# Gate and up by Strassen's seven products, the second norm moved behind the output projection, and the feed-forward in the same program

## The reference, cut to what matters

```python
h = x + mixed @ w_out
gu = rms_norm(h, norm2) @ w_gate_up        # 1024 -> 2 * 2816
gate, up = jnp.split(gu, 2, axis=-1)
return h + (jax.nn.silu(gate) * up) @ w_down
```

## Time and profile before

| | us |
|---|---|
| median of three runs | 3157.95 (3147.9 to 3160.55) |
| the profiled execution's own time | 3149.9 |
| its span, first to last instruction | 3148.2 |
| PE busy | 2934.9 (93%) |
| DVE, ACT, POOL busy | 1575.6, 1087.4, 353.3 |

### The profile page before, as it was taken

How to read it: one execution, slowest core, us unless ns; L and a number is a source line. 1 busy time by engine, 2 the same in 40 slices (tenths; PEclk the granted TensorE clock), 3 DMA queues, 4 the chain that set the end, 5 groups by cost and what they waited for, 6 DMA issues and landing times.

```text
span 3148.2 us, 40326 instructions
## 1 busy us (share of the span) xinstructions
PE 2934.9 (93%) x15304; PEld 2677.0 (85%) x15304; DVE 1575.6 (50%) x2185; ACT 1087.4 (35%) x1792; POOL 353.3 (11%) x389
## 2 busy tenths in 40 slices
PE   5988999899897999958999999899999989999998
PEld 4877889788785888848999999799999979999997
DVE  6765667677466565524433334434334343334343
ACT  4443545354446666623112111312121132121111
POOL 4322111132112232310000000000000000000000
PEclk8999999999997999988999999899999999999999
DMA  5466976765867333323212120512121132121220
GB/s 152 148 211 176 270 206 217 241 195 175 222 181 170 106 93 94 98 80 115 68 53 68 52 80 27 160 54 67 53 80 58 48 120 81 54 80 50 70 67 40
DMA packets 335925, 360.29 MB, mean 114 GB/s; under 512 B 39870, under 2 KB 274878, under 8 KB 335527
## 3 DMA queue, kind: packets, MB, share of 16 engines
q1 hardware_dynamic: 301352, 269.06, 30.7%
q0 software_dynamic: 34464, 89.80, 8.6%
HBM read 273.33 MB, written 85.48 MB: 114 GB/s over the span
## 4 chain that ended last, share of the span: by engine, by line
PE 52%; DMA 1%; DVE 1%; ACT 1%; issue 0%; SPq 0%; POOL 0%; POOLq 0%; DVEq 0%; ACTq 0%
...
## 5 line engine op out<-in xcount | busy, mean ns | idle before, releaser
L83 PE MATMUL ff_acc<-ff_xhi,ff_whi 128*128 128x384 f32 x2112 | 711.3, 337 | 14.8 <-DVE ff_xlo L2428 14.8
L84 PE MATMUL ff_acc<-ff_xlo,ff_whi 128*128 128x384 f32 x2112 | 709.8, 336 | 0.0
L85 PE MATMUL ff_acc<-ff_xhi,ff_wlo 128*128 128x384 f32 x2112 | 709.6, 336 | 0.0
L83 PEld LDWEIGHTS ff_acc<-ff_xhi,ff_whi 128*128 128x128 f32 x2112 | 399.9, 189 | 18.0 <-issue 12.8
L84 PEld LDWEIGHTS ff_acc<-ff_xlo,ff_whi 128*128 128x128 f32 x2112 | 399.9, 189 | 1.2
L85 PEld LDWEIGHTS ff_acc<-ff_xhi,ff_wlo 128*128 128x128 f32 x2112 | 399.6, 189 | 0.0
L2449 DVE TENSOR_TENSOR ff_h<-ff_h,ff_down 128x512 f32<-128x512 f32 x396 | 270.3, 687 | 231.3 <-PE ff_down L85 231.3
L2438 DVE TENSOR_TENSOR ff_prod<-ff_silu,ff_acc 128x384 f32<-128x384 f32 x132 | 73.1, 554 | 599.7 <-ACT ff_silu L2389 599.7
L83 PE MATMUL ff_down<-ff_dhi,ff_ahi 128*128 128x512 f32 x792 | 310.5, 392 | 7.3 <-DVE ff_alo L2441 7.3
L2389 ACT ACTIVATE ff_silu<-ff_acc 128x384 f32<-128x384 f32 x132 | 65.0, 492 | 730.5 <-PE ff_acc L85 730.4
L83 PE MATMUL pr_acc<-pr_xhi,pr_whi 128*128 128x386 f32 (+1 forms) x864 | 304.8, 353 | 7.0 <-DVE pr_xlo L1394 7.0
...
## 6 DMA issues: line engine op xcount, KB each, us to landing
ff_raw<-w_gate_up SPq DMA_DIRECT2D x134, 512.0 KB, 5.1
...
pr_xs<-x SPq DMA_DIRECT2D x36, 512.0 KB, 4.7
f_dram<-fi_out POOLq DMA_DIRECT2D x32, 512.0 KB, 4.1
fs_a<-f_dram SPq DMA_DIRECT2D x32, 512.0 KB, 6.8
...
am_raw<-x SPq DMA_DIRECT2D x18, 512.0 KB, 3.4
```

What stands on the lines that cost most here:

```text
L83: pe.matmul(out, still[0], moving[0], start=start, stop=False)
L84: pe.matmul(out, still[0], moving[1], start=False, stop=False)
L85: return pe.matmul(out, still[1], moving[0], start=False, stop=stop)
```

## The change

The token-by-weight products of a chunk were taken as whole ones. Now the weight block of a chunk, for gate (step s even) and up (s odd), and the token block are each cut into four quarters: 1024 input rows in two halves, 256 hidden channels in two, 768 tokens in two. Strassen's method (Winograd's form) makes four products of quarters from seven multiplications in place of eight, each 4 k-steps x 3 matmuls of 384 columns. Sums of quarters of weights (S1 to S4) are made on POOL for each step, those of tokens (T1 to T4) on DVE and POOL once a group; results are put together by seven DVE additions a step, after a copy by ACT. Gate times up moves from DVE to POOL. The low parts overwrite the raw ones, so a weight buffer can be loaded again only when the products of its step are done, not when it was split.

The norm in front of the feed-forward moves into `mixers`, three iterations behind: ACT squares (`power`) and roots (`root_row`), DVE inverts, POOL scales (`scale_row`), PE turns (`turn_row`), DVE multiplies by the gain (`keep`), SP stores to `xt_dram`. The last tile's is done after the first step's products (`close`). There is one block for all; its feed-forward is written out, not looped. `ahead` starts loads and splits in the last iteration, n = 19. A third of `kk` is given up for space, and loaded later.

```diff
--- before.py
+++ after.py
@@ mixers: sync, gpsimd, tensor, scalar, vector, in this order
...
-            if 2 <= n < NB:
-                bring_h(n)
+            if 3 <= n <= NB:
+                bring_h(n - 1)
+            if n == NB + 1:
+                ahead()
+            if 3 <= n < NB + 2:
+                store_x(n - 3)
...
+        def scale_row(t):
+            pool.wait_ge(recips2, t + 1)
+            if t:
+                pool.wait_ge(x_turned, 2 * t)
+            pool.tensor_scalar(xs[:], hx[:, t % 2, :], scale2[:, t % 2, 2:3], None, ALU.mult).then_inc(scaled2, 1)
+            pool.wait_ge(scaled2, t + 1)
...
+            if n == NB + 1:
+                ahead()
             for i in range(units(n)):
+                if i == 1 and 3 <= n < NB + 2:
+                    scale_row(n - 3)
...
@@ tensor
+        def turn_row(t, q):
+            pe.wait_ge(scaled2, t + 1)
+            b = bank(x_kept, 2 * t + q + 1)
+            for k in range(4):
+                last = pe.transpose(turn[:, b, k * P:(k + 1) * P], xs[:, (4 * q + k) * P:(4 * q + k + 1) * P], ident[:])
+            last.then_inc(x_turned, 1)
...
+                part = turn_at(n, i)
+                if part in (0, 1):
+                    turn_row(n - 3, part)
...
@@ scalar
+        def power(t):
+            act.wait_ge(added, 4 * t + 4)
+            if t:
+                act.wait_ge(x_turned, 2 * t)
+            act.activation(xs[:], hx[:, t % 2, :], ACT.Square, accum_out=scale2[:, t % 2, 0:1]).then_inc(powers, 1)
+
+        def root_row(t):
+            act.wait_ge(powers, t + 1)
+            act.activation(scale2[:, t % 2, 1:2], scale2[:, t % 2, 0:1], ACT.Sqrt, scale=1.0 / D, bias=ones[:, 1:2]).then_inc(rooted2, 1)
...
+                if i == 0 and 3 <= n:
+                    power(n - 3)
                 if i == 0 and mixes(n):
                     root(n - 2)
+                if i == 0 and 3 <= n:
+                    root_row(n - 3)
+                if i == 1 and n == NB + 1:
+                    ahead()
...
@@ feed_forward is gone; swiglu stands in its place
-                    for m in range(2):
-                        for k in range(KT):
-                            o = slice(t * CH, (t + 1) * CH)
-                            last = triple(pe, acc[:, t, m, 0:CH], (whi[:, p, m, k, :], wlo[:, p, m, k, :]), (xhi[:, k, o], xlo[:, k, o]), k == 0, k == KT - 1)
...
+    A11, A12, A22, S3, S1, S2, S4 = range(7)
+    B11, B21, B22, T3, T1, T2, T4 = range(7)
+    STEPS = ((0, A11, B11), (1, S1, T1), (2, S2, T2), (3, A12, B21), (0, S3, T3), (2, A22, T4), (3, S4, B22))
...
+        def run(s):
+            q, p = s // 2, s % 2
+            g, before = q // NC, s - 1
+            for at, (b, w, x) in enumerate(STEPS):
+                if at == 0:
+                    pe.wait_ge(w_low, 2 * s + 1)
+                if at == 1:
+                    pe.wait_ge(w_low, 2 * s + 2)
+                if s == first_of(g):
+                    pe.wait_ge(x_counter(x), (4 if x in X_LOW_DVE else 3) * g + (X_LOW_DVE[x] if x in X_LOW_DVE else X_LOW_POOL[x]))
+                if at < 4 and s:
+                    pe.wait_ge(combined, after(before, (U3, C22, C21, C12)[at]))
+                if at == 4:
+                    pe.wait_ge(copied, s + 1)
+                if at > 4:
+                    pe.wait_ge(combined, after(s, U2 if at == 5 else C11))
+                for k in range(4):
+                    last = triple(pe, bank(b), (whi[p][:, w, k, :], wlo[p][:, w, k, :]), (xhi[x][:, k, :], xlo[x][:, k, :]), k == 0, k == 3)
+                last.then_inc(multiplied, 1)
+
+        def lower(q):
...
@@ swiglu, gpsimd
+        def sums(s):
+            q, p = s // 2, s % 2
+            raw = wraw[p]
+            pool.wait_ge(w_in[p], 64 * (q + 1))
+            if s >= 2:
+                pool.wait_ge(multiplied, step_done(s - 2, 6))
+            pool.tensor_tensor(raw[:, S1], raw[:, S3], raw[:, A22], ALU.add).then_inc(w_summed, 1)
...
@@ swiglu, scalar
+        def weight_high(s, part):
+            q, p = s // 2, s % 2
+            if part == 0:
+                act.wait_ge(w_in[p], 64 * (q + 1))
+                if s >= 2:
+                    act.wait_ge(multiplied, step_done(s - 2, 5))
+                act.copy(whi[p][:, 0:3], wraw[p][:, 0:3]).then_inc(w_high, 1)
+            else:
+                act.wait_ge(w_summed, 4 * s + 4)
+                act.copy(whi[p][:, 3:7], wraw[p][:, 3:7]).then_inc(w_high, 1)
...
@@ swiglu, vector
+        def corner(s, c):
+            q, p = s // 2, s % 2
+            if c == C22:
+                dve.wait_ge(combined, after(s, U3))
+            else:
+                dve.wait_ge(multiplied, step_done(s, {C11: 3, C21: 5, C12: 6}[c]))
+            if p == 0 and q:
+                dve.wait_ge(tempered, 4 * (q - 1) + 1 + TURN[c])
+            if p:
+                at_least(dve, lowered, NV * q)
+            to = block(prod, c) if p else silu[c][:]
+            one, b = {C11: (r1, 3), C22: (u2, 1), C21: (u2, 2), C12: (v5, 3)}[c]
+            dve.tensor_tensor(to, one[:], bank(b), ALU.add).then_inc(combined, 1)
...
+        def weight_low(s, part):
+            p, o = s % 2, slice(0, 3) if part == 0 else slice(3, 7)
+            dve.wait_ge(w_high, 2 * s + 1 + part)
+            dve.wait_ge(w_summed, 4 * s + 4)
+            dve.tensor_tensor(wlo[p][:, o], wraw[p][:, o], whi[p][:, o].bitcast(F32), ALU.subtract).then_inc(w_low, 1)
...
+                if c == 0 and q:
+                    row_sum(g, T1)
+                    add(q - 1, 0)
+                    add(q - 1, 1)
+                    row_sum(g, T2)
+                    row_sum(g, T4)
+                    add(q - 1, 2)
+                    add(q - 1, 3)
+                    for n, x in enumerate((B11, T1, T2, T4)):
+                        row_low(g, x)
+                        add(q - 1, 4 + 2 * n)
+                        add(q - 1, 5 + 2 * n)
+                    weight_low(2 * q + 1, 0)
+                    weight_low(2 * q + 1, 1)
+                second(2 * q)
...
@@ swiglu, tensor, main
+            for q in range(NQ):
+                c = q % NC
+                if c == 0 and q:
+                    lower(q - 1)
+                run(2 * q)
+                if q == 0:
+                    close()
+                    pe.wait_ge(mix_added, 4 * NTT)
+                    pe.wait_ge(x_kept, 2 * NTT)
+                if c:
+                    lower(q - 1)
+                run(2 * q + 1)
+            lower(NQ - 1)
+
```

711 lines of the change are left out of this document (459 added, 252 removed).

## The result

| | before | after |
|---|---|---|
| median us (runs) | 3152.93 (4) | 3034.38 (4), 3033.5 to 3037.52 |
| profiled span | 3148.2 | 3032.9 |
| PE clock, mean granted | 0.966 | 0.966 |

A forecast was written before the change was run, and what follows sets the result against it. PE, busy 93% of the span, was taken as the bound, with losses at crossings. Mixers' end 1411.5 + first crossing 50 + chunks 1501.8 + turns 2 x 23 + end 10.3 = 3019.6 us span; predicted 3025, range 2970 to 3065.

The forecast's parts named there:

- products and chunk: Feed-forward chunks: 168 matmuls of 384 columns for 192, 4.16 us less each, 137 in all; a chunk takes 45.51 us.
- waits inside chunks: Feed-forward chunks: PE waits for no other engine inside them; 33 x 45.51 = 1501.8 us.
- mixers: Mixers: turned groups add 15 us on PE, the later root on ACT 13; last matmul at 1383.5 + 28 = 1411.5.
- first crossing: From the mixers' last matmul into the feed-forward: 50 us lost, chunk 0's 7 included, against 56.8 before.
- a turn: Between groups: lowering starts 5 late and ends 11.8 late, gate step 4 more, chunk 0 7; 23 us, was 27.5.
- Rival (5): Chunks: PE's gain eaten by starts of 14 short accumulations a chunk, 0.3 us each, so no change; chance 0.03.
- The slack in the up step: Up step with the next gate step: DVE's work is ready 1.3 to 3 us before PE wants it.
- (3): Up step's slack of 1.3 us used up, a wait in every chunk; at 1 us late each 3058; chance 0.15.
- (4): Up step: DVE later by more than 5.2 us in each chunk, slower than before, 3201 at 51 a chunk; chance 0.05.
- Taking turns of DVE and POOL: Quarter passes at the crossings: two-operand work of both doesn't overlap; 1536 columns take 3.5 us on POOL, 1.75 on DVE.
- Rival (2): Crossings are short because passes on POOL and DVE overlap or fall apart in time; 2993 us; chance 0.2.
- Chunk 0: First chunk of each group: DVE's weight splits are ready later than wanted; PE loses 4.3 + 2.6 = 7 us.

The follow-up runs named there:

- e1_eighth: Changed kernel with every step's seventh product computed twice, so a chunk has the 192 matmuls of before again: 3160.74 us, ratio 1.0032 to before.
- e10_twice: Changed kernel with PE turning each of the eight blocks of a tile's row twice, 16 transposes for 8: 3046.82 us, ratio 0.9671 to before.
- e3_table: Changed kernel with one more Sqrt of a constant column on ACT ahead of a row's squaring, to load the table earlier: 3023.46 us, ratio 0.9591 to before.
- e13_accum: Changed kernel with DVE's seven quarter passes of a group reading one operand and writing out an accumulator, output not the reference's: 3018.74 us, ratio 0.9582 to before.
- e4_pool_first: Changed kernel with POOL scaling tile 16 ahead of the gate weights' sums in the mixers' last iteration: 3033.24 us, ratio 0.9620 to before.
- e5_chunk0: Changed kernel with the next gate weights cast and split earlier on ACT and DVE in each group's first chunk: 3008.09 us, ratio 0.9546 to before.

## Why the prediction was right, step by step

The median came out at 3034.4 for 3025, the profiled span 13.3 us above the sum's 3019.6. By its own steps:

| step | forecast us | measured | off |
|---|---|---|---|
| products and chunk | 45.51 a chunk | 45.61 | +3.3 |
| waits inside chunks | none | none | 0 |
| mixers | +28 | +24.1 | -3.9 |
| first crossing | -6.8 | -6.5 | +0.3 |
| a turn | 23, was 27.5 | 28.3 and 27.0, were 27.4 and 26.8 | +10.0 |
| start of the last lowering | 0 | +1.8 | +1.8 |
| behind the last lowering | 0 | -4.6 | -4.6 |
| front | 0 | +2.9 | +2.9 |
| what the sum missed of before's span | | 3.5 | +3.5 |

The mixers are measured over 16 iterations and forecast over all 17 tiles; what lies behind the last root counts in the first crossing. How the measured ones come out: a turn is the distance of two lowering starts less 11 chunks (529.96 - 501.7 = 28.3), the second with 2.3 us added, since the last lowering waits 4.1 and not 6.4; before, 573.8 and 573.2 less 546.4. The first crossing is what is left of the stage: -137.7 is 33 x -4.06, +1.0 for the turns, +1.8, and -6.5.

- **Products.** Right, and e1_eighth shows them to be the whole gain. The 0.10 us a chunk may be starts of accumulations; no run shows it. Rival (5) needed 0.3 us for each of 14, some 4 us a chunk.
- **The slack in the up step** was there; no wait has the count of the chunks. Rivals (3) and (4) didn't come, though what (3) named is there: POOL's products take 1.49 us in the mean for the 1.02 forecast, so DVE and POOL take turns in the chunks too, within the slack.
- **Mixers.** Both mechanisms right. Transposes 0.86 us an iteration for 0.88 (e10_twice), the late root 0.85 by the rows (3.25 for 2.4), of which e3_table could take away 0.55 an iteration. An inner iteration is 1.7 longer for 1.73; over all 16, of which the last are short, 24.1 / 16 = 1.51.
- **Taking turns of DVE and POOL.** Right for two-operand passes: of DVE's 21 quarter passes ten are held up, to 2.6 to 5.0 us, and eleven take 1.75. POOL's take 3.53 alone (taken: 3.5) and 4.9 beside DVE. Worth 16 us by e13_accum. Rival (2), short crossings, fell with it. Its finer half, that additions from accumulators pass, holds: they have a mean of 685 ns over 396, no longer than in the earlier trace rows, and none takes more than 692.
- **First crossing.** The net came out by luck of two errors, the places right. Counted from the last root, the gate step ended at 53.1 for 56.5 and the up step at 81.7 for 84.2; against that stand 3.2 us of starts at half clock behind chunk 0's stops, which weren't counted. The wait for tile 16's row came as forecast in kind, but was 16.2 us: the sums went on to 19.3 and not 16.3, and the scaling behind them took 4.41 beside DVE (2.84 alone) where 1.2 was taken; the bound of 2.6 from POOL's own rows was nearer than DVE's. T1 came at 37.6 (forecast 38). The wait was worth nothing: without it, in e4_pool_first, T1 came at 32.7, and the gate step ended at 53.7.
- **Chunk 0** waited 8.2 and 8.3 us at the turns and 7.0 at the first crossing for the 7 forecast, right in place and, for two thirds of it, in cause (e5_chunk0: 7.9 of 23.5 us stay).
- **A turn** is the mis-sized term. Forecast were 5 + 6.8 + 4 + 7, 22.8 us of stops. Measured in the first, start to start: lowering 6.7, the additions 2.0 + 2.3, ACT's copy 2.5, chunk 0 6.5 + 2.5; less the regular distances 21.4. The waits below are those rows of PE's timeline.

```profile
1970.07 0.50 PE L85 MATMUL ff_down<-ff_dhi,ff_ahi 128*128 128x512 f32 x1 [1.64 <-DVE ff_h L2725]
...
1975.04 0.50 PE L85 MATMUL ff_down<-ff_dhi,ff_ahi 128*128 128x512 f32 x1 [1.93 <-DVE ff_h L2725]
...
1988.56 0.42 PE L85 MATMUL ff_banks<-ff_xhi,ff_ghi 128*128 128x384 f32 x1 [2.11 <-ACT ff_r L2593]
...
2016.17 0.69 PE L85 MATMUL ff_banks<-ff_xhi,ff_ghi 128*128 128x384 f32 x1 [6.19 <-DVE ff_glo L2713]
...
2022.33 0.69 PE L85 MATMUL ff_banks<-ff_xhi,ff_ghi 128*128 128x384 f32 x1 [1.96 <-DVE ff_glo L2713]
```

  The stops were forecast well in sum (the additions and the copy too high, the start and chunk 0 too low). Left out is the clock: behind the two long stops PE's starts are 0.32 and 0.43 us apart, at the lower of the two levels of the granted clock (1.2 for 2.4 GHz), 7.2 and 5.5 us a turn. The prediction counted that in the first crossing alone, although the 27.5 us of the turn before, from which it went out, hold 4.9 of it.
- **The tail.** Left out: y's last 512 KB went by POOL's queue before and go by SP's now. From the last matmul's start to the end of the span 9.0 us before, 4.2 after. No run has the one without the other, so the queue as cause isn't shown.
